# A hybrid decoder step: channel mixing in three token parts with the samples beside the prompt, an fp32 column-tiled down product for the sample rows, and another order of the projection groups

## The reference, cut to what matters

```python
z = rms_norm(x, g_attn) @ w_in                      # 2840 columns: qa | cmp | slc | win | gate | qb | kb | vb
...
x = x + o @ w_o
h = rms_norm(x, g_ffn)
a = h @ w_gate
ext = concat([conv_prev, a], axis=1)                # the two tokens before; zeros for the prompt
c = conv_b + sum(conv_w[k] * ext[:, k:k + S] for k in range(3))
y = x + (silu(c) * (h @ w_up)) @ w_down
```

## Time and profile before

| what | value |
|---|---|
| runs | 2011.82 to 2014.28 us, median 2013.63 us |
| the profiled execution | 2008.03 us; span from first to last instruction 2006.2 us |
| TensorE matmuls (PE) | busy 1879.5 us, 94% of the span |
| VectorE (DVE), ScalarE (ACT), GpSimd (POOL) | busy 52%, 38%, 13% |
| granted TensorE clock, mean | 0.98 |
| `project` | first product at 36 us, `prepare` starts at 338 us |
| `finish` | output projection from 1038 us, channel mixer from 1150 us to the end |

### The profile page before, as it was taken

The page is one execution under the profiler, slowest core; times in us unless marked ns, Lnnn a source line. Parts: engine busy times, 40 slices in busy tenths (PEclk is TensorE's granted clock), DMA queues, the critical chain, the costliest instruction groups (busy, mean ns, idle before and its releaser), DMA issues. The chain is left out here.

```text
span 2006.2 us, 30543 instructions
## 1 busy us (share of the span) xinstructions
PE 1879.5 (94%) x11675; PEld 1494.0 (74%) x11675; DVE 1044.3 (52%) x2481; ACT 761.9 (38%) x1583; POOL 263.8 (13%) x344
## 2 busy tenths in 40 slices
PE   5997999979999899899969999999999999999997
PEld 4786777977776666666647787787887887887886
DVE  5866881336666666666644435434434434433434
ACT  4444442116777565655542332212212212212211
POOL 1000000004444344443310000000000000000000
PEclk7998999999999999999989999999999999999999
DMA  5334232415655322233352213113113113114102
GB/s 181 108 110 134 87 113 90 160 34 144 176 169 163 99 91 87 90 90 101 100 182 86 63 42 106 63 42 105 63 43 105 63 42 105 64 42 147 41 3 93
DMA packets 171942, 192.09 MB, mean 96 GB/s; under 512 B 55302, under 2 KB 138502, under 8 KB 169528
## 3 DMA queue, kind: packets, MB, share of 16 engines
q1 hardware_dynamic: 169458, 175.56, 28.1%
q0 software_dynamic: 2352, 14.73, 2.2%
HBM read 168.72 MB, written 59.81 MB: 114 GB/s over the span
## 5 line engine op out<-in xcount | busy, mean ns | idle before, releaser
L1847 DVE CUSTOM_DVE_ANT_0 l_e<-l_s,k_masks 128x1024 f32<-128x1024 f32 (+3 forms) x192 | 138.5, 721 | 102.7 <-PE l_s L1492 101.6
L1792 ACT ACTIVATE l_e<-l_e,l_nmin 128x640 f32<-128x640 f32 (+11 forms) x224 | 169.0, 754 | 32.5 <-DVE l_nmin L1847 30.8
L2267 PE MATMUL o_py<-f_h_hi,m_gu_hi 128*128 128x512 f32 x704 | 179.7, 397 | 0.0
L2267 PE MATMUL o_py<-f_h_lo,m_gu_hi 128*128 128x512 f32 x704 | 178.5, 395 | 0.0
L2267 PE MATMUL o_py<-f_h_hi,m_gu_lo 128*128 128x512 f32 x704 | 178.4, 395 | 0.0
L2267 PEld LDWEIGHTS o_py<-f_h_hi,m_gu_lo 128*128 128x128 f32 x704 | 132.1, 188 | 32.2
L2267 PEld LDWEIGHTS o_py<-f_h_lo,m_gu_hi 128*128 128x128 f32 x704 | 132.0, 188 | 32.2
L2267 PEld LDWEIGHTS o_py<-f_h_hi,m_gu_hi 128*128 128x128 f32 x704 | 129.7, 188 | 29.7
L2525 DVE SCALAR_TENSOR_TENSOR a_kv_nat<-m_ext,m_taps,a_kv_nat 128x512 f32<-128x512 f32 x22 | 16.6, 752 | 249.9 <-ACT m_ext L2416 249.9
L1532 PE MATMUL l_t<-k_ident,l_e 128*128 128x128 f32 x816 | 123.7, 276 | 0.5 <-POOL l_e L1439 0.3
L375 PE MATMUL p_pz<-p_whi,p_xhi 128*128 128x512 f32 (+3 forms) x432 | 104.6, 386 | 19.9 <-DVE p_xlo L407 15.7
(11 more groups left out here) (312 smaller groups left out, 3695.9 us busy)
## 6 DMA issues: line engine op xcount, KB each, us to landing
m_raw_gu<-in_w_gate SPq DMA_DIRECT2D x22, 512.0 KB, 5.2
m_raw_gu<-in_w_up SPq DMA_DIRECT2D x22, 512.0 KB, 7.0
m_raw_d<-in_w_down SPq DMA_DIRECT2D x11, 1024.0 KB, 5.0
k_first<-in_w_in SPq DMA_DIRECT2D x5, 2048.0 KB, 8.1
a_kd_k<-in_state_dil SPq DMA_DIRECT2D x8, 1024.0 KB, 8.2
a_kd_v<-in_state_dil SPq DMA_DIRECT2D x8, 1024.0 KB, 7.7
a_kd_k<-in_cache_slc SPq DMA_DIRECT2D x128, 64.0 KB, 1.8
k_w<-in_w POOLq DMA_DIRECT2D x4, 1024.0 KB, 5.6
```

The source lines that it names most:

```text
L1792: nc.scalar.activation(e, e, ACT.Exp, bias=nmin[0:r, k:k + 1], scale=-1.0, accum_out=total[0:r, k:k + 1]).then_inc(exped, 1)
L1847: return nc.vector.tensor_tensor_reduce(out=dst, in0=src, in1=m, scale=1.0, scalar=CLAMP, op0=ALU.add, op1=ALU.min, accum_out=low)
L2267: last = nc.tensor.matmul(bank[q % 3][:, 0:w], ws[k][:, m, c, :], hs[:, c, t0:t0 + w], start=(j == 0 and c == 0), stop=(j == 2 and c == KC ...
```

## The change

In `project` the group `win_gate` moves from the third place of the table to the sixth. Nothing else of that stage is edited; what counts groups or tiles (the waits of GpSimd, the buffer of a tile) counts in the new order.

In `finish` the samples no longer have parts of their own. A chunk's 1088 tokens are taken in three parts of 384, 384 and 320, where the last has 256 prompt and the 64 sample tokens. `part_s`, `turn_s`, their bank and their ScalarE copy go. A part uses one of two pairs of banks in turn, and waits for the `g_made` of the second part before it. The down units of the pair before stand after parts 0, 1 and 2 (7, 6 and 4 of them). The sample rows' down product is one unit: four float32 matmuls with the unsplit product `m_g_s` (64 columns, stationary) and the unsplit weights `m_raw_d` (moving); the two halves of the outputs go to partitions 0 to 63 and 64 to 127 of one bank. For that, the second half of the samples' `x` is moved to partitions 64 to 127 once. `m_raw_d` is now loaded for a pair when the sample unit of the pair before is done. In the last pair the split of part 3 stands ahead of part 4.

```diff
 GROUPS = [
     ("qa", 0, 512, (2, 4), (0, 1)),
     ("cmp_slc", 512, 512, (2, 2), (1, 3)),
-    ("win_gate", 1024, 280, (1, 2), (3, 4)),
...
     ("vb", 2328, 512, None, None),
+    ("win_gate", 1024, 280, (1, 2), (3, 4)),
...
-PARTS = [(0, 512), (512, 512), (SEQ, NS)]
+PARTS = [(0, 384), (384, 384), (768, 320)]
...
-        UNITS_D = 2 * STEPS
+        UNITS_D = 2 * TILES + 1
...
-        DOWN = [*range(0, 8), 16, 17, *range(8, 16)]
-        DOWN_AFTER = {0: range(0, 10), 2: range(10, 18)}
+        DOWN = [*range(0, 6), 16, *range(6, 16)]
+        DOWN_AFTER = {0: range(0, 7), 1: range(7, 13), 2: range(13, 17)}
...
+            sp.wait_ge(y_added, STEPS)
+            sp.dma_start(x[NS:P, TILES, 0:HALF], x[0:NS, TILES, HALF:D]).then_inc(x_moved, 16)
...
+                if i > 0:
+                    sp.wait_ge(d_filled, (i - 1) * UNITS_D + DOWN.index(2 * TILES) + 1)
+                    load_wd(i)
...
-                    sp.wait_ge(wd_lo_done, i + 1)
-                    load_wd(i + 1)
...
             def part(i, q):
-                if q >= 3 or i > 0:
-                    pe.wait_ge(g_made, i * NP + (q - 2))
+                if i > 0 or q >= 2:
+                    pe.wait_ge(g_made, i * NP + q - 1)
...
-                            last = nc.tensor.matmul(bank[q % 3][:, 0:w], ws[k][:, m, c, :], hs[:, c, t0:t0 + w], ...
+                            last = nc.tensor.matmul(bank[q % 2][:, 0:w], ws[k][:, m, c, :], hs[:, c, t0:t0 + w], ...
...
+                    if d == 6:
+                        pe.wait_ge(g_made, i * NP + NP)
...
+                    if tile == TILES:
+                        for k in range(2):
+                            for x in range(2):
+                                last = nc.tensor.matmul(down_bank(i, d)[x * NS:(x + 1) * NS, :], g_s[:, k, :], raw_d[:, k, x * HALF:(x + 1) * HALF],
+                                                        start=(k == 0), stop=(k == 1))
...
             def body(i, first, last):
-                part(i, 0)
...
-                turn_s(i, 1)
+                for q in range(NP):
+                    part(i, q)
+                    if first and q == 0:
+                        turn_h(STEPS - 1)
+                    if not first and q in DOWN_AFTER:
+                        down(i - 1, DOWN_AFTER[q])
...
-                        split_g(i, q - 1)
+                        if not (last and q == 4):
+                            split_g(i, q - 1)
...
+                    if last and q == 3:
+                        split_g(i, 3)
```

More of the change, by code:

```diff
@@ L2189, in _ @@
                 else:
-                    sp.dma_start(o["y_sample"].rearrange("b s d -> (b s) d"), x[0:NS, n, :]).then_inc(y_out, 16)
+                    for half in range(2):
+                        sp.dma_start(o["y_sample"].rearrange("b s d -> (b s) d")[:, half * HALF:(half + 1) * HALF],
+                                     x[half * NS:(half + 1) * NS, n, 0:HALF]).then_inc(y_out, 16)
             sp.wait_ge(kept_rows, 6)
@@ L2301, in down @@
+                    if d in (0, 7, 13):
+                        pe.wait_ge(g_lo_done, i * NP + {0: 4, 7: 5, 13: 6}[d])
                     pe.wait_ge(d_added, i * UNITS_D + (d + 1))
-                    for n in range(6):
-                        k, j = n // 3, n % 3
-                        a, w = ((g_hi, wd_hi), (g_hi, wd_lo), (g_lo, wd_hi))[j]
-                        last = nc.tensor.matmul(pd[d % 3][0:r, :], a[:, k, tok], w[:, k, hs], start=(n == 0), stop=(n == 5))
+                    if tile == TILES:
[3 more added lines that the diff above has]
+                                                        start=(k == 0), stop=(k == 1))
+                    else:
+                        for n in range(6):
+                            k, j = n // 3, n % 3
+                            a, w = ((g_hi, wd_hi), (g_hi, wd_lo), (g_lo, wd_hi))[j]
+                            last = nc.tensor.matmul(down_bank(i, d), a[:, k, tile * P:(tile + 1) * P], w[:, k, half * HALF:(half + 1) * HALF],
+                                                    start=(n == 0), stop=(n == 5))
@@ L2306, in down @@
                     last.then_inc(d_filled, 1)
             def body(i, first, last):
-                part(i, 0)
-                if first:
-                    turn_h(STEPS - 1)
-                    part(i, 1)
-                    part_s(i, 0)
-                else:
-                    down(i - 1, DOWN_AFTER[0])
-                    part_s(i, 0)
-                    part(i, 1)
-                turn_s(i, 0)
-                if not first:
-                    down(i - 1, DOWN_AFTER[2])
-                part(i, 3)
@@ L2508, in add @@
                     tile, half = DOWN[d] // 2, DOWN[d] % 2
-                    r = P if tile < TILES else NS
-                    xs = x[0:r, tile, half * HALF:(half + 1) * HALF]
+                    xs = x[:, tile, half * HALF:(half + 1) * HALF]
+                    if i == 0 and tile == TILES:
+                        dve.wait_ge(x_moved, 16)
                     dve.wait_ge(d_filled, i * UNITS_D + (d + 1))
-                    nc.vector.tensor_tensor(xs, pd[d % 3][0:r, :], xs, ALU.add).then_inc(d_added, 1)
+                    nc.vector.tensor_tensor(xs, down_bank(i, d), xs, ALU.add).then_inc(d_added, 1)
             def body(i, first, last):
@@ L2535, in body @@
                     if not first:
-                        add(i - 1, {0: range(2, 10), 1: range(11, 12), 2: range(13, 18)}.get(q, ()))
-                    if q > 0:
+                        add(i - 1, {0: range(2, 7), 1: range(9, 13), 2: range(15, 17)}.get(q, ()))
+                    if q > 0 and not (last and q == 4):
                         split_g(i, q - 1)
```

109 lines of the change are left out of this document (44 added, 65 removed).

## The result

The changed kernel takes 1947.34 us (median of 4 runs, 1945.89 to 1947.66) where the kernel before takes 2012.72 (4 runs, 2010.18 to 2014.28): a ratio of 0.9675, 95% interval 0.9663 to 0.9686, or 65.4 us less. Forecast were 1956 us, range 1940 to 1979. The profiled execution of the changed kernel took 1947.66 us, its span 1945.5; against the profiled one of before (2008.03) that is 60.4 us less. The working of the forecast was made between profiled executions, so its 57.5 us stand against these 60.4.

A forecast was written before the change was run, and what follows sets the result against it. TensorE's own work was taken to bound the kernel. Gate and up -33, samples' down product -9, last pair's end -4.5 and group order -11 sum to -57.5 us: 2013.6 to 1956 us, range 1940 to 1979.

The forecast's parts named there:

- gate and up: Gate and up matmuls of each channel-mixer pair: 288 at 177 and 149 ns, 48.3 us for 51.3, -33 us in 11 pairs.
- the group order: Moving `win_gate` last in `project`: removes its wait for the next group's weights, less new costs, -11 us (bounds -4, -16).
- What bounds the kernel: Middle pair of the channel mixer: TensorE busy 76.00 of 76.00 us, so only the sum of its own work counts.
- the straight line: Matmul cost interpolated between 129 ns at 280 columns and 233 at 512: 176 ns at 384, 147 at 320.
- the upper bound: Matmul cost as columns at 2.4 GHz plus a fixed 20 ns: 180 ns at 384 columns, 153 at 320.
- The samples' down unit: Samples' down product in each pair: four float32 matmuls in 1.9 us for two units' 2.74, -9 us in 11 pairs.
- `attend`'s pairs: Float32 matmuls alternating between partition halves overlap: six of 256 columns take 1.45 us where one after the other takes 2.6.
- Rival 2: Sample unit's two halves don't overlap: 3.6 us in place of 1.9, 11 times, +19 us, 1975 us; chance 0.09.
- The waits: Waits that could open in the mixer, for banks, adds or weights: all covered, shortest cover 7.2 against 4.6 us, cost nothing.
- The end of the last pair: Idle time before the last pair's first down unit goes, 1.8 us before the fourth stay: -4.5 us (bounds -1, -6).
- the barrier: End of `project`: the last tile, now a narrow one, must be normed and rotated ahead of the barrier, 3 us more.
- Rival 1: Weight loads of 188 ns don't overlap and pace every part matmul: 2.8 us more a pair, 2020 us; chance 0.06.

## Why the prediction was right, and where it was off

The sum came nearer than its terms: gate and up gave 8 us more than forecast, the group order 3 less, and the stages without an edit took 2.4 back.

**What bounds the kernel** held: TensorE's own work, without a gap in a pair, before and after.

**Gate and up** was forecast at -33 us and is -41 (51.3 - 47.6 = 3.7 us in each of 11 pairs). The step that failed is the choice of 177 and 149 ns, between the straight line and the upper bound, for the reason that the 280-wide rows came from another stage. They were good rows: line and proportion gave 175 to 176 and 146 to 147, and 174.6 and 146.7 is what came. Two or three ns on 288 matmuls and 11 pairs are the 8 us. The run with extra matmuls shows why the line was safe here: 280 columns and 512 lie on the same side of the bend. Had the nearest row below been 128 columns wide, a line from it would have been wrong.

**The samples' down unit** was forecast at 1.9 us and is 1.87, -9.6 us in all for -9. The argument from `attend`'s pairs was right, and the run in one half shows the cause and its price, 19 us by 11 x (3.58 - 1.87). Rival 2 would have been 20 us.

**The waits** at nothing: right, and with room, as the parts of 448 show.

**The end of the last pair** was -4.5, and is -5.0 (5.9 less the 0.87 of the shorter sample unit). The number was right and its cause wrong: the step "the change puts that split ahead of part 4, so the first unit follows part 5 directly" credits a move that is worth nothing. The part that stands there now hides the split in either place. The stall ahead of the fourth unit came as forecast, if smaller, 1.2 us for 1.8.

**The group order** was -11 and is -8.3 between the traces, 9.4 between medians. The narrow group went from 45.4 to 32.1 us, -13.3 where -14.6 and +2 were put; the barrier costs 2.1 more where 3 were put. One step failed: the sentence that `vb` and its neighbours keep their lengths, since 512-wide tiles cover loads and splits. With `qb`'s slow start they were to give 1.5 back and took 3.0 instead, 1.3 of it in `kb` (its wait of 2.38 us) and 0.8 in `cmp_slc`, which now splits 512-wide weights for its successor where it split 280. Wide tiles don't cover a load of 8 us: ScalarE waits 3.3, 1.8 and 4.3 us for one. Another step, "the tiles are too short to cover a 2 MB load", left out a part: of the 8.6 us some 5 are that, and some 3.5 are GpSimd's load beside it, as the times from issue to landing show. In the last place there is no successor's load or split, so the term needed no division of the wait, and its size came near.

**Rival 1**, the weight loads: if it is they that set the floor, which is not shown, their pace is 110 ns and not 188, so they bind only below some 240 columns. The loads of the narrow matmuls still last 192 ns each; nearly two of them run at a time.

**The medians** fell 5 us more than the profiled executions. The stage whose length differs most between executions without an edit is `attend`: 586.6 us in the profiled execution of before, the shortest of fourteen, and 586.8 to 592.7 in the others, the changed kernel's 588.5 among them. That accounts for some 2 us. The kernel before took 2005.5 to 2015.9 us in the runs beside the experiments, so a single execution of it can lie 5 us off; no more than that is known of the rest.

## What to carry to other kernels

Before moving work between matmuls of different widths, find the width below which the cost no longer falls, by rows of both sides of it: above it only the sum of columns counts and operands can be merged or cut freely, below it only the number of matmuls. A stall that a change is meant to remove can be hidden by another part of the same change, so undo each part alone before crediting it. And where an engine waits for a load, look at two times separately, the load's from issue to landing and the engine's from the issue until it comes to the data: the first tells whether another queue's traffic slowed the load, the second what the tiles cover. A shorter wait alone can mean that the engine came later.

## What the runs showed of the hardware

- Float32r matmuls with 128 stationary columns, new weights each time, start 108 to 111 ns apart at 64, 128 and 192 columns, and 0.456 ns a column apart from 256 to 512, at a granted clock of 1.00 (2.4 GHz), where a column alone would be 0.417 ns.
- Four float32 matmuls of 64 stationary and 512 moving columns take 1.87 us on two halves of the partitions and 3.58 on one. With two halves their order in the queue makes no difference: a matmul of the free half starts ahead of one that stands before it.
- A 2 MB load took 11.6 us from issue to landing with a 1 MB load issued 0.24 us ahead of it on another queue, and 8.1 us with that load issued 6.5 us ahead.
- Loads of 128 float32r columns last 187 to 192 ns in the records, and a stream with one ahead of each narrow matmul starts a matmul every 110 ns, so nearly two loads are under way at a time.
- `attend`, which no edit touched, took 586.6 to 592.7 us in fourteen profiled executions.
